# Side work between weight split and eviction, and sample states updated by VectorE alone, in a two-layer hybrid decoder step

## What is computed

```python
h = rmsnorm(x) * (1 + sc1) + sh1
z, xbc, dt_raw, u, v, ga, gb = split_cols(h @ w_in, IN_SIZES)
ya, hs, cs = ssd_branch(z, xbc, dt_raw, ...)          # conv, silu, chunked state space scan, gated norm
yb, vr = chunk_mlp_branch(gelu(u), gelu(v), ...)      # layernorm of v, spatial matrix per 128 tokens
merged = sigmoid(ga) * (ya @ w_ssd_out) + sigmoid(gb) * (yb @ w_cmlp_out)
x = x + g1 * rmsnorm(merged @ w_o)
```

## Time and profile before

| | us |
|---|---|
| median of 3 runs | 1922.27 |
| lowest and highest | 1920.86, 1924.54 |
| the profiled execution, its own time | 1918.96 |
| span of its profile, first to last instruction | 1917.1 |
| mixer of layer 0 in the profile: chunk z0 to the second chunk of ssd_out | 103.76 to 361.69 |
| the same in layer 1 | 733.03 to 965.81 |

### The profile page before, as it was taken

How to read it: one execution, slowest core, us unless ns; L and a number is a source line. 1 busy time by engine, 2 the same in 40 slices (tenths; PEclk the granted TensorE clock), 3 DMA queues, 4 the chain that set the end, 5 groups by cost and what they waited for, 6 DMA issues and landing times.

```text
span 1917.1 us, 33371 instructions
## 1 busy us (share of the span) xinstructions
PE 1758.5 (92%) x13192; PEld 1636.8 (85%) x13192; DVE 1340.9 (70%) x1318; ACT 1038.0 (54%) x1063; POOL 116.6 (6%) x128
## 2 busy tenths in 40 slices
PE   6998999869999969989796999999999999999994
PEld 4887898768999869889795999989898989899993
DVE  3765456754444488765756788878887888788884
ACT  2445545323333334664342776767676777677771
POOL 4022101000000002310100000000000000000000
PEclk8999998989999979999896999999999999999996
DMA  9987542337886436662240999999999999999980
GB/s 274 293 264 256 174 155 89 121 123 228 278 286 213 144 99 188 209 193 95 88 147 18 340 352 345 350 301 351 347 350 312 334 351 347 335 318 352 344 314 23
DMA packets 379498, 465.09 MB, mean 243 GB/s; under 512 B 10404, under 2 KB 351604, under 8 KB 379379
## 3 DMA queue, kind: packets, MB, share of 16 engines
q1 hardware_dynamic: 372370, 441.65, 70.4%
q0 software_dynamic: 6720, 20.86, 3.4%
q10 hardware_dynamic: 304, 1.08, 0.2%
HBM read 452.84 MB, written 10.92 MB: 242 GB/s over the span
## 4 chain that ended last, share of the span: by engine, by line
PE 81%; DVE 9%; ACT 5%; issue 3%; DMA 2%; POOL 0%; DVEq 0%; SPq 0%; ACTq 0%; POOLq 0%
PE psum L404 10%; PE psum L415 10%; PE psum L409 9%; PE psum L1204 9%; PE psum L1209 9%; PE psum L1206 9%; PE psum L1228 4%; PE psum L1232 4%; PE psum L1229 4%; PE psum L444 2%; PE psum L762 2%; ACT whi L343 1%; DVE wlo L348 1%; PE psum L1163 1%; PE psum L1180 1%
## 5 line engine op out<-in xcount | busy, mean ns | idle before, releaser
L370 DVE TENSOR_TENSOR wlo<-raw,whi 128x2048 fp32r<-128x2048 f32 x219 | 501.6, 2292 | 107.8 <-ACT whi L365 107.0
L348 DVE TENSOR_TENSOR wlo<-raw,whi 128x2048 fp32r<-128x2048 f32 x113 | 264.8, 2344 | 266.3 <-ACT whi L343 266.0
L365 ACT ACTIVATE whi<-raw 128x2048 fp32r<-128x2048 f32 x219 | 418.4, 1912 | 31.6 <-PE psum L1232 30.0
L404 PE MATMUL psum<-xhi,whi 128*128 128x264 f32 x1584 | 243.7, 310 | 51.4 <-ACT xhi L1292 40.5
L404 PEld LDWEIGHTS psum<-xhi,whi 128*128 128x128 f32 x1584 | 220.5, 206 | 72.3 <-issue 59.4
L343 ACT ACTIVATE whi<-raw 128x2048 fp32r<-128x2048 f32 x113 | 216.6, 1917 | 92.9 <-PE psum L415 72.4
L409 PE MATMUL psum<-xlo,whi 128*128 128x264 f32 x1584 | 214.4, 289 | 0.0
L415 PE MATMUL psum<-xhi,wlo 128*128 128x264 f32 x1584 | 214.3, 289 | 0.0
L409 PEld LDWEIGHTS psum<-xlo,whi 128*128 128x128 f32 x1584 | 206.1, 195 | 0.0
L1204 PE MATMUL psum<-whi,hghi 128*128 128x256 f32 x1408 | 202.2, 286 | 3.1 <-issue 2.2
L415 PEld LDWEIGHTS psum<-xhi,wlo 128*128 128x128 f32 x1584 | 201.2, 191 | 0.0
(11 more groups left out here) (360 smaller groups left out, 1939.9 us busy)
## 6 DMA issues: line engine op xcount, KB each, us to landing
raw<-in_exp_wd_dram SPq DMA_DIRECT2D x76, 1024.0 KB, 5.0
raw<-in_exp_wg_dram SPq DMA_DIRECT2D x72, 1024.0 KB, 6.6
raw<-in_exp_wu_dram SPq DMA_DIRECT2D x72, 1024.0 KB, 6.7
raw<-in_w_in_dram SPq DMA_DIRECT2D x52, 1024.0 KB, 5.3
raw<-in_w_mod_dram SPq DMA_DIRECT2D x17, 1024.0 KB, 5.3
hf<-in_exp_wu_dram SPq DMA_DIRECT2D x16, 1024.0 KB, 6.2
hf<-in_exp_wg_dram SPq DMA_DIRECT2D x16, 1024.0 KB, 6.4
hf<-in_exp_wd_dram SPq DMA_DIRECT2D x12, 1024.0 KB, 5.0
```

Of the source, the lines that this page charges most:

```text
L348: dve.tensor_tensor(wlo[slot], raw[slot], whi[slot].bitcast(F32), ALU.subtract) \
L365: act.activation(whi[j % R3], raw6[slot], ACT.Copy).then_inc(sem["hi_ready"], 1)
L370: dve.tensor_tensor(wlo[j % R3], raw6[slot], whi[j % R3].bitcast(F32), ALU.subtract) \
L404: pe.matmul(out, whi[slot][:, k, j * P:(j + 1) * P], hi(k), start=first and k == 0, stop=False)
```

## The change

1. **ACT.** `after` is gone from `act_phase`; all side work moves to `ahead`, so it stands behind the split of chunk c+1 and before the eviction of chunk c. The outer products lie ahead of the evictions z3, v0, v2, v3, u1, u2, ga0, ga1. The second silu of the convolution stands between the phases z and v.
2. **PE and DVE** have the side work on other chunks: the broadcast of the samples after z2, z3, v1, v2, u0, u1, u3, ga0; DVE's `sample` after v0, v1, v3, u0, u2, u3, ga1, ga2. The turning of B and C moves from after z2 to after z1.
3. **The layernorm of v**: gain and bias for four of the eight feature tiles go to DVE as `tensor_scalar`.
4. **The states**: POOL no longer multiplies. DVE does decay and addition in one fused form, eight operations of 128 elements per sample, and waits itself for the landing of the state. POOL fetches states 0 and 1 first, then 2.
5. **gb and cmlp_out**: `tokens(0)` and `segments(0)` one chunk earlier on DVE, the copy of B (`keep_b`) before the eviction; the multiplication of ce by C on DVE inside `masked(1)`; `masked(1)` before the split of chunk cmlp 3.
6. **ssd_out**: DVE finishes the prompt's state after the gated norm instead of before it, PE turns it after chunk 0 of ssd_out instead of before it, ACT copies it ahead of the end of chunk 1. The loops of PE and ACT over ssd_out are written out.
7. A semaphore of its own for one output copy, with no other effect on the order.

```diff
@@ act_phase
-                    if after:
-                        after(c + 2 * i)
@@ pool, per layer
-                def decay(b):
-                    pool.wait_ge(s_in[b % SR3], 16 * (l * PER[b % SR3] + b // SR3 + 1))
-                    pool.tensor_tensor(sring[b % SR3], sring[b % SR3], bc(spx[:, :, b], 2, [P, KT, NS]), ALU.mult) \
-                        .then_inc(sem["samp_decayed"], 1)
-                pool.wait_ge(sem["w_turned"], l + 1)
-                fetch_state(2)
                 pool.wait_ge(sem["tail_out"], 32 * (l + 1))
                 fetch_state(0)
                 fetch_state(1)
-                for b in range(SR3):
-                    decay(b)
+                pool.wait_ge(sem["w_turned"], l + 1)
+                fetch_state(2)
...
-                for g in (1, 0):
-                    pool.wait_ge(sem["ce_exp"], 2 * (l + 1) - g)
-                    ins = pool.tensor_tensor(ce[:, g * R:(g + 1) * R, :], ce[:, g * R:(g + 1) * R, :],
-                                             bc(xcv[:, KT + G + g, Q:2 * Q], 1, [P, R, Q]), ALU.mult)
-                ins.then_inc(sem["ce_ready"], 1)
@@ tensor
-                    if c == 3:
-                        sample_rows(0)
+                    if c >= 2:
+                        sample_rows(c - 2)
+
+                def after_v(c):
+                    if c == 1 or c == 2:
+                        sample_rows(c + 1)
...
-                    if c == 1:
-                        sample_rows(5)
+                    if c < 2:
+                        sample_rows(4 + c)
+                    if c == 3:
+                        sample_rows(6)
...
-                    if c < 2:
-                        sample_rows(6 + c)
+                    if c == 0:
+                        sample_rows(7)
                     if c == 1:
-                        pe.wait_ge(sem["v_normed"], l + 1)
+                        pe.wait_ge(sem["v_normed"], 2 * (l + 1))
                         turn_v(0, 2)
@@ scalar
+                def ahead_z(c):
                     if c == 1:
                         act.wait_ge(sem["conv_done"], l + 1)
                         act.activation(xcv[:, :, S:T], xcv[:, :, S:T], ACT.Silu).then_inc(sem["xc_ready"], 1)
+                        act.wait_ge(sem["tail_turned"], l + 1)
+                        act.activation(tail[0:CK - 1 + B, 0:CD], msf[0:CK - 1 + B, 0:CD], ACT.Copy).then_inc(sem["tail_ready"], 1)
                     if c == 2:
                         act.wait_ge(sem["bc_turned"], l + 1)
                         act.wait_ge(sem["bc_zero"], l + 1)
                         act.activation(bct[0:B, :], ms[0:B, 2, :], ACT.Copy).then_inc(sem["bc_ready"], 1)
+                        act.wait_ge(sem["conv_part"], 9 * l + 5)
+                        act.activation(xcv[:, 0:7, 0:S], xcv[:, 0:7, 0:S], ACT.Silu)
                     if c == 3:
-                        act.wait_ge(sem["conv_part"], 9 * l + 9)
-                        act.activation(xcv[:, 7:CT, 0:S], xcv[:, 7:CT, 0:S], ACT.Silu)
-                        outer(0)
+                        sample(0)
+                def ahead_v(c):
+                    if c == 0:
+                        sample(1)
+                    if c >= 2:
+                        sample(c)
+                def ahead_u(c):
+                    if c == 1 or c == 2:
+                        if c == 2:
+                            act.wait_ge(sem["v_centered"], l + 1)
+                            act.activation(hf[:, :, :], vb[:, :, :], ACT.Square).then_inc(sem["v_sq"], 1)
+                        sample(3 + c)
+                def ahead_ga(c):
+                    if c == 0:
+                        sample(6)
                     if c == 1:
                         act.wait_ge(sem["v_root"], l + 1)
-                        for t in range(KT):
+                        for t in range(HT, KT):
...
+                        sample(7)
+                    if c >= 2:
+                        act.wait_ge(sem["v_tok"], l * NQ + c - 1)
+                        act.activation(vtok[:, c - 2, :], msf[:, 1024:2048], ACT.Copy).then_inc(sem["v_tok_ready"], 1)
@@ vector
                     dve.wait_ge(sem["outer_ready"], l * B + b + 1)
-                    dve.wait_ge(sem["samp_decayed"], l * B + b + 1)
-                    dve.tensor_tensor(Sb, Sb, sprod[s], ALU.add).then_inc(sem["s_new"], 1)
+                    dve.wait_ge(s_in[b % SR3], 16 * (l * PER[b % SR3] + b // SR3 + 1))
+                    for k in range(KT):
+                        ins = dve.scalar_tensor_tensor(out=Sb[:, k, :], in0=Sb[:, k, :], scalar=spx[:, k, b:b + 1],
+                                                       in1=sprod[s][:, k, :], op0=ALU.mult, op1=ALU.add)
+                    ins.then_inc(sem["s_new"], 1)
...
+                        dve.wait_ge(sem["v_root"], l + 1)
+                        for t in range(HT):
+                            ins = dve.tensor_scalar(vb[:, t, :], vb[:, t, :], row("cmlp_ln_g", l, t),
+                                                    row("cmlp_ln_b", l, t), ALU.mult, ALU.add)
+                        ins.then_inc(sem["v_normed"], 1)
...
+                    if c == 1:
+                        tokens(0)
                     if c == 2:
-                        tokens(0)
-                    if c == 3:
                         segments(0)
...
                     for g in (1, 0):
+                        if c:
+                            dve.wait_ge(sem["ce_exp"], 2 * (l + 1) - g)
+                            ins = dve.tensor_tensor(ce[:, g * R:(g + 1) * R, :], ce[:, g * R:(g + 1) * R, :],
+                                                    bc(xcv[:, KT + G + g, Q:2 * Q], 1, [P, R, Q]), ALU.mult)
...
                 segments(1)
+                masked(1)
                 split_lo(dve, n + 3, 0)
-                masked(1)
                 cmlp_chunk(2)
...
-                dve.wait_ge(sem["last_ready"], (l + 1) * NQ)
-                hv = hT[:, :].rearrange("p (h d) -> p h d", h=H)
-                then(dve.tensor_tensor(hv, hv, bc(elast[:, :], 2, [P, H, HD]), ALU.mult))
-                dve.wait_ge(sem["st_part"], (l + 1) * NQ)
-                dve.tensor_tensor(hT[:, :], hT[:, :], msf[:, 1024:2048], ALU.add).then_inc(sem["st_ready"], 1)
                 for g, ks in enumerate(HALVES):
...
                 lo_of_x(5 * l + 3, hf)
+                dve.wait_ge(sem["last_ready"], (l + 1) * NQ)
...
+                dve.tensor_tensor(hT[:, :], hT[:, :], msf[:, 1024:2048], ALU.add).then_inc(sem["st_ready"], 1)
```

More of the change, by code:

```diff
@@ L472, in mod_keep, with act_phase @@
                 .then_inc(sem["mod_added"], 1)
-        def act_phase(act, key, count, epilogue=None, peel=0, end=False, after=None, ahead=None):
+        def act_phase(act, key, count, epilogue=None, peel=0, end=False, ahead=None):
             n0, q0 = N0[key], Q0[key]
@@ L489, in body @@
                         epilogue(i, c, acc[:, 2 * pair:2 * pair + 2, 0:T]).then_inc(acc_free[pair], 1)
-                    if after:
-                        after(c + 2 * i)
-            loop(act, count // 2, body, count // 2 if end or after or n0 <= MB else peel)
+            loop(act, count // 2, body, count // 2 if end or ahead or n0 <= MB else peel)
         def dve_phase(dve, key, count, epilogue=None, peel=0, cols=T, end=False, after=None):
@@ L1357, in outer, with sample @@
                     ins.then_inc(sem["outer_ready"], 1)
-                def after_z(c):
-                    if c == 0:
-                        act.wait_ge(sem["tail_turned"], l + 1)
-                        act.activation(tail[0:CK - 1 + B, 0:CD], msf[0:CK - 1 + B, 0:CD], ACT.Copy).then_inc(sem["tail_ready"], 1)
+                def sample(b):
+                    outer(b)
+                def ahead_z(c):
                     if c == 1:
@@ L1881, in after_u @@
                     if c == 2:
-                        sample(5)
+                        sample(4)
                     if c == 3:
@@ L1885, in after_u @@
                         mean_inv(rs[:, 0, :], ms[:, 2, 0:T], D, sem["v_inv"])
+                        sample(5)
                 def after_ga(c):
```

98 lines of the change are left out of this document (48 added, 50 removed).

## The result

| | before | after | forecast |
|---|---|---|---|
| median of 4 runs, us | 1922.74 | 1869.93 | 1880 (1868 to 1897) |
| lowest and highest | 1920.86, 1924.54 | 1868.67, 1872.05 | |
| profiled execution | 1918.96 | 1868.83 | 1876.5 |
| span of its profile | 1917.1 | 1867.1 | |

The ratio is 0.9727, with a 95% interval of 0.971 to 0.9743. The kernel is 52.8 us faster where 42.5 were forecast; the time lies inside the range, 10 us under the likeliest value. First the chain that ended last, from the page of the kernel after (part 4): PE's share has gone from 81% to 89%.

What follows compares the result with a forecast made beforehand. PE was taken as the bound (81% of the chain), through idle time and low clock. 19.7 + 13.2 + 2 × (1.8 + 3.0) = 42.5 us off 1918.96 gave 1876.5, as a median 1880, range 1868 to 1897.

Steps and rivals of the forecast that it cites:

- A: The forecast itself: the change works as worked out, 1873 to 1887 us, chance 0.72.
- ACT's order: Mixers' v, u and ga: with the split first, stretches fall to busy time; 19.7 us layer 0, 13.2 layer 1.
- States, no cost: Eight fused operations on DVE take 2.15 us, a sample 4.7; PE loses nothing, or 0.1 us, in layer 1.
- Landings: DVE's waits for states stay hidden: 8.9 us from issue, 13 us at the least until use, 4 us spare.
- gb: `spread_cum(0)` no longer waits for B: 1.8 us per layer, bounds 1.0 and 2.0.
- Gains of the layernorm: At ga1 and ga2: half the gains, 2.0 us, stays on ACT; DVE takes four operations, 2.2 us, side by side.
- the clock in the tail: Matmuls behind the shorter wait run more at full clock, up to 1.4 us; 3.0 taken per layer, net 2.6.
- The masks: In cmlp_out: masks take about 2.4 instead of 4.53 us, 2.1 us sooner for PE's wait of 3.27.
- ssd_out: Moving two DVE operations behind the reciprocal gives 1.6 us; PE's turning of the state inside the path costs 1.1.
- C: Side work itself waits, so only the end of POOL's multiplying counts: 10 us gained, 1912 us, chance 0.07.
- B: DVE gates PE: layer 1's broadcasts (4 us), ga's root, gain, turn (up to 2 per layer); 1894 us, chance 0.15.
- D: Slower: DVE waits for state landings with low parts behind it, PE waits too; 1930 us at 23 us landings, chance 0.04.

Runs made afterwards that it cites:

- x2: The changed kernel with ACT's side work before the split of chunk c+1 again in phases z, v, u and ga; 1906.85 us.
- x7: The changed kernel with eight more fused operations of 128 elements per sample on DVE; 1884.78 us.
- x6: The changed kernel with DVE's `tokens(0)` and `segments(0)` back behind the low parts of gb 2 and gb 3; 1873.25 us.
- x4: The changed kernel with all eight layernorm gains on ACT, none on DVE; 1877.18 us.
- x9: The changed kernel once more, unedited; 1870.44 us.
- x5: The changed kernel with DVE's finishing of the prompt's state before the gated norm and PE's turning before ssd_out again; 1872.96 us.
- x3: The kernel before with only the states changed: DVE scales and adds in eight fused operations, GpSimd multiplies no state; 1909.08 us.
- x1: The changed kernel with GpSimd multiplying the states by their decays again and DVE adding in one operation; 1877.88 us.
- x8: The changed kernel with every refetch of a state issued one sample later; 1873.19 us.
- x11: The changed kernel with the multiplication of the exponents by C back on GpSimd, masks still first on DVE; 1872.63 us.
- x12: The changed kernel with the low part of cmlp 3 ahead of DVE's multiplications and masks again, GpSimd silent; 1873.8 us.
- x10: The changed kernel with y of block 1 taken up earlier, squares summed inside cmlp 3, root's table loaded earlier; 1869.73 us.

## Why the prediction was right, point by point

**The likeliest case, A, came true in its mechanism.** Its signs came: v0 of layer 0 under 8.6 us, ga1 with ga2 under 15 at clock 1.00, the fused operations in 2.17 us, the masks in 1.23 and 1.22; the mixers gained 29.4 and 20.9 us where some 24 and 18 were expected. Most of the forecast's terms can be read off against the profile.

- *ACT's order, 32.9 us.* From z0 to gb 0 layer 0 gained 21.4 us (19.7 forecast) and layer 1 14.5 (13.2); x2 gives the size, some 32, and the cause. The surplus in the trace is small: ga1 and ga2 take 13.50 us where 14.7 was the sum, and v1 to v3 of layer 0 24.09 where 25.71 was their busy time, since broadcasts now fall into z and u3, which grew (z0 to z3 of layer 0 by 1.0 us).
- *States, no cost.* 2.17 us per eight, 2.15 forecast; a sample takes 4.75 us from the first fused operation to the end of the reduce (144.11 to 148.86), 4.7 forecast. The prediction's tight places in layer 1 were real: x7 loses 3.5 us there, where 4 were priced. The estimate of 2.33 us from the formula of the Trainium skill, VectorE: DVE Perf Modes, section on the TRN2 errata, is 7% above the 2.17, and its advice for tiles of 512 elements and more does not carry over to this choice: two plain operations of 1.22 us on 1024 elements would be 2.44, more than the eight.
- *Landings.* DVE never waited. The shortest way from a refetch to its use was 14.6 us (state 3 of layer 1, issued at 749.09 and used at 763.73), where 13 were counted; the median landing of a state there was 6.3 to 7.7 us, where 8.9 were taken.
- *gb.* 2.06 and 1.87 us in gb 2 for a forecast of 1.8. The step named the right cause, B, which ACT copies; x6 shows that DVE's half adds nothing.
- *Gains of the layernorm.* Right in direction, inside the 6.4 and 6.9 us of ga1 and ga2; x4 gives their own part, 1.2 us per layer.

**Where the 10 us came from.** The profiled executions differ by 50.1 us, 7.6 more than forecast; the other 2.2 are that I set the median 3.3 us above the profile, and it lies 1.1 above. Up to gb 0 the mixers gave 3.0 us more than the 32.9. To gb and the tail I gave 9.6 us in both layers, and from gb 0 to the end of w_o 0 they gave 9.4 and 7.9, 17.3, which is 7.7 more; the rest of the kernel took 3.1 back, 1.5 of it in layer 1's last chunk of xbc (7.39 instead of 5.92 us, clock 0.78), where eight of the experiments did not. The term that was too small is the clock in the tail, the 0.4 us per layer by which I took 3.0 and not 2.6.

- *The clock.* Of the 7.7 us, 5.8 lie in gb 3 and w_o 0, with the same idle time of PE: 2.1 + 0.7 and 1.5 + 1.5 us in this trace. I had allowed "up to 1.4" for the matmuls behind the tail's wait, a figure for which no row was given, and nothing for gb 3 and w_o 0. Behind the masks the end of cmlp 2 took 6.78 us at a clock of 0.75 before (330.53 to 337.31) and 5.11 at 1.00 after (303.95 to 309.06), 1.7 more. x9 shows that the same kernel loses part of it again, so it is no steady part of the gain: in so far the surplus is luck.
- *The masks* came 2.4 us sooner for the 2.1 forecast, so their sum was right. The multiplications that come in and the split that goes out are not quite "near cancelling": beside GpSimd that split had taken 3.40 us and not the 2.34 counted, and against it DVE now stands idle 0.77 us for ACT's exponentials ahead of the first mask. DVE before:

```profile
322.62 3.40 DVE L348 TENSOR_TENSOR wlo<-raw,whi 128x2048 fp32r<-128x2048 f32 x1
```

- *ssd_out*, 0.5 us per layer, does not show: cmlp 3 to ssd 1 took 30.2 us in both layers before, 29.9 and 30.3 after. Only x5 shows that the move is worth something once the masks come sooner.

**The rivals.** C (only GpSimd's silence counts, 1912 us) is x3, with 1909.08: its price at v0, 3.0 us per layer, was too low, 5.4 and 4.8. GpSimd had slowed the multiplication ahead of the convolution too (1.92 instead of 0.41 us), and the silu came 4.5 us sooner, not 3.0; x1 shows the same of a low part, with 3.52 us. B had one of its two places right and its sum low by half. D was far off: x8 delayed the landings until DVE waited, and PE lost 2.0 us in all. The Trainium skill, SBUF — State Buffer, section Who interferes with whom, says that a VectorE instruction with two inputs in SBUF contends with a GpSimd instruction that reads SBUF, and that the second blocks until the first is done. The trace of x11 agrees: GpSimd's second multiplication ran from 301.66 for 2.49 us, to 304.15; the mask issued at 302.56 ended at 305.24, 1.09 us after it, about the 1.22 that it takes alone.

## What to carry to other kernels

Put what the next stage waits for (here the weight split) first on its engine, and fill the wait behind it with side work: this swap alone was worth 32 us by the stretches and 37 by the medians, more than all the arithmetic moved. An operation that goes to another engine is judged there by the cover at its place; the same multiplications cost 12 us in one order and some 2 in another. A wait that has gone from a trace may only mean that the waiting engine came later: look at its clock, and at the end of the work that it waits for. When a step's gain is under some 4 us, read the stretch and not the median, and compare the stretch in several traces of kernels that are the same there.

## What the runs showed of the hardware that I had not expected

PE's clock falls at the same places in some executions and not in others. In gb 3 of layer 0, behind 32 small matmuls (16 rows by 128 columns, 3.83 us) and with no idle time of PE in the chunk before, the chunk took 7.40 us in the changed kernel and in x12, and 8.92 to 8.99 us in x1, x2, x4, x5, x6, x8, x9, x10 and x11; with x9 that is one kernel with both (granted clock 1.00 and 0.81). w_o 0 of layer 0, behind idle time of 1.26 us in the chunk before, took 6.83 us in the changed kernel, x2, x4, x8 and x11 and 8.26 to 8.41 us in the other seven of the new order. The trace that I read thus had good fortune in both places. Why one execution keeps the clock and another not is open; no run tried to prevent it.
